# Attention scores as three 64-row products per head pair instead of two stacked 128-row products

## What is computed

```python
def cross_attend(q, k, v):
    n, t, _ = q.shape
    q = q.reshape(n, t, C_HEADS, C_HEAD_DIM)
    s = jnp.einsum('nthd,nshd->nhts', q, k.astype(q.dtype)).astype(jnp.float32) * (C_HEAD_DIM ** -0.5)
    p = jax.nn.softmax(s, axis=-1).astype(q.dtype)
    o = jnp.einsum('nhts,nshd->nthd', p, v.astype(q.dtype))
    return o.reshape(n, t, C_WIDTH)
```

## Time and profile before

| | us |
|---|---|
| median of 3 runs | 405.94 |
| profiled execution | 405.82 |
| its span | 404.1 |
| TensorE matmul busy | 396.3 (2406 instructions) |
| weight loads busy | 371.2 (2406) |
| DVE / ACT / POOL busy | 221.7 / 201.3 / 125.9 |
| granted TensorE clock, mean | 0.998 |

### The profile page before, as it was taken

The page is one execution under the profiler, slowest core; times in us unless marked ns, Lnnn a source line. Parts: engine busy times, 40 slices in busy tenths (PEclk is TensorE's granted clock), DMA queues, the critical chain, the costliest instruction groups (busy, mean ns, idle before and its releaser), DMA issues.

```text
span 404.1 us, 6121 instructions
## 1 busy us (share of the span) xinstructions
PE 396.3 (98%) x2406; PEld 371.2 (92%) x2406; DVE 221.7 (55%) x306; ACT 201.3 (50%) x339; POOL 125.9 (31%) x73
## 2 busy tenths in 40 slices
PE   8999999999999999999999999999999999999994
PEld 8999899999999999999999999999998688888883
DVE  4998696534377668557499734945546241111112
ACT  5974737655446536668694228448163231122220
POOL 2024732232333333203470304205024224444420
PEclk9999999999999999999999999999999999999999
DMA  7993040111012011100350501404342302321122
GB/s 256 411 415 136 0 157 2 54 52 52 0 52 57 6 45 53 52 2 0 115 199 3 208 2 54 156 2 138 107 138 102 105 1 104 104 103 68 72 73 104
DMA packets 13061, 37.96 MB, mean 94 GB/s; under 512 B 2112, under 2 KB 2632, under 8 KB 12912
## 3 DMA queue, kind: packets, MB, share of 16 engines
q1 hardware_dynamic: 13040, 37.68, 26.3%
HBM read 32.84 MB, written 4.83 MB: 93 GB/s over the span
## 4 chain that ended last, share of the span: by engine, by line
PE 95%; DMA 2%; SPq 1%; DVE 1%; ACT 0%; issue 0%; DVEq 0%
PE ps L385 52%; PE ps L655 22%; PE ps L447 3%; DMA mixT<-in_xT 2%; PE ps L589 2%; PE ps L497 2%; PE ps L567 2%; PE ps L555 2%; PE ps L475 1%; PE ps L477 1%; PE ps L489 1%; PE ps L488 1%; PE ps L666 1%; PE ps L668 1%; PE ps L624 1%; PE ps L539 1%
## 5 line engine op out<-in xcount | busy, mean ns | idle before, releaser
L385 PE MATMUL ps<-x_hi,w_hi 128*128 128x344 f32 x456 | 148.8, 326 | 0.5 <-DVE x_lo L1123 0.5
L385 PE MATMUL ps<-x_hi,w_lo 128*128 128x344 f32 x456 | 145.7, 319 | 0.0
L385 PE MATMUL ps<-x_lo,w_hi 128*128 128x344 f32 x456 | 145.5, 319 | 0.0
L385 PEld LDWEIGHTS ps<-x_hi,w_hi 128*128 128x128 f32 x456 | 85.8, 188 | 1.0 <-DVE x_lo L1123 0.8
L385 PEld LDWEIGHTS ps<-x_lo,w_hi 128*128 128x128 f32 x456 | 85.7, 188 | 0.1
L385 PEld LDWEIGHTS ps<-x_hi,w_lo 128*128 128x128 f32 x456 | 85.7, 188 | 0.0
L985 POOL TENSOR_TENSOR w_lo<-w_stage,w_hi 128x1024 fp32r<-128x1024 f32 x17 | 41.7, 2456 | 137.4 <-ACT w_hi L692 127.3
L655 PE MATMUL ps<-x_hi,w_hi 128*128 128x512 f32 x128 | 50.6, 395 | 0.0
L655 PE MATMUL ps<-x_lo,w_hi 128*128 128x512 f32 x128 | 50.5, 394 | 0.0
L655 PE MATMUL ps<-x_hi,w_lo 128*128 128x512 f32 x128 | 50.5, 394 | 0.0
L1092 DVE TENSOR_TENSOR zT<-ps,rstdB 128x344 f32<-128x344 f32 x33 | 16.8, 513 | 34.0 <-PE ps L385 34.0
(11 more groups left out here) (231 smaller groups left out, 650.0 us busy)
## 6 DMA issues: line engine op xcount, KB each, us to landing
w_stage<-in_w_tiles SPq DMA_DIRECT2D x17, 512.0 KB, 3.3
mixT<-in_xT SPq DMA_DIRECT2D x8, 516.0 KB, 8.1
x_ring<-in_x_all SPq DMA_DIRECT2D x8, 512.0 KB, 4.0
o_y<-zT SPq DMA_DIRECT2D x7, 512.0 KB, 2.9
zT<-in_w_out SPq DMA_DIRECT2D x5, 512.0 KB, 4.5
zT<-in_w_mem SPq DMA_DIRECT2D x4, 512.0 KB, 10.9
zT<-in_kcT SPq DMA_DIRECT2D x8, 256.0 KB, 4.0
zT<-in_vc SPq DMA_DIRECT2D x8, 256.0 KB, 5.6
```

Of the source, the lines that this page charges most:

```text
L385: last = pe.matmul(ps[:, bank, 0:GN], w[:, slot, wk], xx[:, k, cols], start=(x == 0 and n == 0), stop=(x == KT - 1 and n == 2))
```

## The change

The stacked copies go. `k_hi`, `k_lo`, `q_hi` and `q_lo` keep the natural layout (both heads of a tile on their own 64 partitions), each made by one 128-partition instruction. A score is three matmuls over 64 rows, hi x hi, hi x lo and lo x hi (the product of the two low parts is left out). Within a tile `t` the two heads alternate, head 0 on rows 0 to 63 into bank 3 and head 1 on rows 64 to 127 into bank 4. A pass has 2 x 3 x 2 = 12 matmuls. The waits count one instruction where they counted two or four, and POOL's wait on itself goes. Each of the four new views takes 512 columns of `z_r`; nothing is placed in `x_r` for the keys any more.

```diff
--- before.py
+++ after.py
@@ -158,11 +158,10 @@
 
 
         z_r, x_r = over("z_r", Z0 + 8 * TT, [P, 3 * TT]), over("x_r", XR0, [P, 2 * TT])
-        k_hh = z_r[:, 0:1024].rearrange("p (a b n) -> p a b n", a=2, b=2)
-        q_st = z_r[:, 1024:2048].rearrange("p (u a b n) -> p u a b n", u=2, a=2, b=2)
+        k_hi, k_lo = (z_r[:, 512 * n:512 * (n + 1)].rearrange("p (t m) -> p t m", t=2) for n in range(2))
+        q_hi, q_lo = (z_r[:, 512 * n:512 * (n + 1)].rearrange("p (u t n) -> p u t n", u=2, t=2) for n in (2, 3))
         v_z = [t.rearrange("p (h n) -> p h n", h=NH) for t in (
             z_r[:, 2 * TT:2 * TT + NH * 3 * HD], x_r[:, 0:NH * 3 * HD])]
-        k_ll = x_r[:, TT:TT + 1024].rearrange("p (a b n) -> p a b n", a=2, b=2)
         xc_hi, xc_lo = (z_r[:, 0:TT], z_r[:, 2 * TT:3 * TT], s_r1[:, :]), x_r[:, 0:TT]
         strips = (x_r[:, TT:2 * TT], s_r1[:, :], x_r[:, TT:2 * TT])
         probsT_hi = over("probsT_hi", PT0, [P, 1024])
@@ -459,8 +458,8 @@
             gemm(3, 1, 1)
             gemm(3, 2, 1)
 
-            pe.wait_ge(khi_done, 4)
-            pe.wait_ge(klo_done, 4)
+            pe.wait_ge(khi_done, 1)
+            pe.wait_ge(klo_done, 1)
             pe.wait_ge(vlo_done, 4)
             pe.wait_ge(const_set, 9)
 
@@ -481,14 +480,15 @@
             with pe.Fori(0, 4) as i:
                 for u in range(2):
                     m, s = i * 2 + (ATT0 + u), i * 2 + u
-                    pe.wait_ge(qc_done, s * 2 + 2)
+                    pe.wait_ge(qc_done, s + 1)
                     for t in range(2):
-                        for hh in range(2):
-                            out = ps[:, 3 + hh, t * NM:(t + 1) * NM]
-                            pe.matmul(out, q_st[:, u, hh, t, :], k_hh[:, hh, t, :], start=True, stop=False)
-                            last = pe.matmul(out, q_st[:, u, hh, t, :], k_ll[:, hh, t, :], start=False, stop=True)
-                            if t == 1:
-                                last.then_inc(sc_done, 1)
+                        for n, (q, k) in enumerate(((q_hi, k_hi), (q_hi, k_lo), (q_lo, k_hi))):
+                            for hh in range(2):
+                                r = slice(hh * HD, (hh + 1) * HD)
+                                last = pe.matmul(ps[:, 3 + hh, t * NM:(t + 1) * NM], q[r, u, t, :], k[r, t, :],
+                                                 start=(n == 0), stop=(n == 2))
+                                if t == 1 and n == 2:
+                                    last.then_inc(sc_done, 1)
                     gemm(m, 0, u)
                     gemm(m, 1, u)
                     for b in range(2):
@@ -748,19 +748,13 @@
 
             def split_q(c0, slot):
 
-                for hh in range(2):
-                    r = slice(hh * HD, (hh + 1) * HD)
-                    act.activation(q_st[r, slot, hh, :, :], zT[r, 0:2, bass.ds(c0, P)], ACT.Copy).then_inc(qhi_done, 1)
+                act.activation(q_hi[:, slot, :, :], zT[:, 0:2, bass.ds(c0, P)], ACT.Copy).then_inc(qhi_done, 1)
 
             act.wait_ge(q_done, 2)
             split_q(0, 0)
             act.wait_ge(kTp_done, 1)
-            for src in range(2):
-                for hh in range(2):
-                    r, to = slice(hh * HD, (hh + 1) * HD), (hh + src) % 2
-                    act.activation(k_hh[to * HD:(to + 1) * HD, hh, :, :],
-                                   ps[r, 5, :].rearrange("p (t n) -> p t n", t=2), ACT.Copy,
-                                   scale=-HD ** -0.5).then_inc(khi_done, 1)
+            act.activation(k_hi, ps[:, 5, :].rearrange("p (t n) -> p t n", t=2), ACT.Copy,
+                           scale=-HD ** -0.5).then_inc(khi_done, 1)
             for j in range(2):
                 act.wait_ge(z_used, 3 * (T_GC + j + 1))
                 act.activation(sig_c[j], mixT[:, 6 + j, :], ACT.Sigmoid).then_inc(gcsig_done, 1)
@@ -1012,14 +1006,11 @@
             with pool.Fori(0, 4) as i:
                 for u in range(2):
                     m, s = i * 2 + (ATT0 + u), i * 2 + u
-                    pool.wait_ge(qhi_done, s * 2 + 2)
+                    pool.wait_ge(qhi_done, s + 1)
 
                     pool.wait_ge(wlo_done, m + 1)
-                    for hh in range(2):
-                        r, to = slice(hh * HD, (hh + 1) * HD), slice((1 - hh) * HD, (2 - hh) * HD)
-                        pool.tensor_tensor(q_st[to, u, hh, :, :], zT[r, 0:2, bass.ds(i * (2 * P) + u * P, P)],
-                                           q_st[r, u, hh, :, :].bitcast(F), ALU.subtract).then_inc(qc_done, 1)
-                        pool.wait_ge(qc_done, s * 2 + (hh + 1))
+                    pool.tensor_tensor(q_lo[:, u, :, :], zT[:, 0:2, bass.ds(i * (2 * P) + u * P, P)],
+                                       q_hi[:, u, :, :].bitcast(F), ALU.subtract).then_inc(qc_done, 1)
                     low_w(m + 1, 1 - u)
 
             pool.wait_ge(wsT_in, 16)
@@ -1159,13 +1150,9 @@
                 for odd in range(2):
                     dve.tensor_tensor(z[:, odd, :, 0:HD] if odd else z[:, odd, :, 2 * HD:3 * HD], v[:, odd, :, :],
                                       z[:, odd, :, HD:2 * HD].bitcast(F), ALU.subtract).then_inc(vlo_done, 1)
-            dve.wait_ge(khi_done, 4)
-            for hh in range(2):
-                r = slice(hh * HD, (hh + 1) * HD)
-                for to in range(2):
-                    dve.scalar_tensor_tensor(k_ll[to * HD:(to + 1) * HD, hh, :, :],
-                                             ps[r, 5, :].rearrange("p (t n) -> p t n", t=2), -HD ** -0.5,
-                                             k_hh[r, hh, :, :].bitcast(F), ALU.mult, ALU.subtract).then_inc(klo_done, 1)
+            dve.wait_ge(khi_done, 1)
+            dve.scalar_tensor_tensor(k_lo, ps[:, 5, :].rearrange("p (t n) -> p t n", t=2), -HD ** -0.5,
+                                     k_hi.bitcast(F), ALU.mult, ALU.subtract).then_inc(klo_done, 1)
 
             def gate_c(j):
                 dve.wait_ge(gcsig_done, j + 1)
```

## The result

The changed kernel takes 407.39 us (407.33 to 407.59, 7 runs) against 405.94 us before on the same chip: a ratio of 1.0034, 95% interval 1.0024 to 1.0044. It is slower by 1.45 us where 407.1 was forecast. The profiled execution took 407.35 us, its span is 405.6 us, 1.5 us longer than before.

A forecast was written before the change was run, and what follows sets the result against it. TensorE's own stream was taken to bound the kernel. Per pass, -0.23 us from paired scores and +0.39 from form changes give +0.16, over eight passes +1.25: 405.82 + 1.25 = 407.1 us, range 403.8 to 412.4.

The forecast's parts named there:

- TensorE's stream alone sets the end: From 15.15 to 398.7 us TensorE is busy without a hole; changes to its stream move the end one for one.
- Part 1: Score matmuls: six overlapping half-row pairs at 0.117 us gain 0.23 us per pass; one after another they lose 0.39.
- C: Rival, score blocks: pairs overlap and the form change is free, -0.23 us per pass, 403.9 us; chance 0.16.
- B: Rival, score blocks: weight loads queue and form changes cost, +0.78 us per pass, 412.0 us; chance 0.25.
- D: Rival, score blocks: weight loads queue, form change free, +0.39 us per pass, 408.9 us; chance 0.08.
- Part 2: Between w_in products and scores: changing from 128 rows to 64 and back costs 0.39 us per pass.
- bound of 0: Low end for the form changes: none, since lines 666 and 668 alternate 64 and 32 columns without a gap.
- Part 3: ACT, DVE and POOL: fewer copies and subtractions free time but end no TensorE wait, so worth nothing.
- The sum: Eight passes of -0.23 + 0.39 = +0.16 us give +1.25 us on the path, 407.1 us.
- E: Rival, score blocks: half-row loads aren't hidden under any matmul, +2.02 us per pass, 422 us; chance 0.05.

## Why the prediction was right, point by point

- *TensorE's stream alone sets the end.* Right. The other engines lost 17 us of busy time together and gave nothing back, and the experiments moved by what their TensorE streams moved.
- *Part 1, a pair costs one full matmul.* Right: steps of 0.12 us, head 1 free (407.32 without it), 0.116 us per pair by the run with hi x hi alone. It was a choice between two ends, not a derivation: the prediction gave this one 0.62 between forecast and C, and no row of the kernel before has products of two row halves side by side. In the changed kernel's second block two loads have started 0.07 us after its start, where a second load of the same half comes after 0.11. Why both halves load together no run shows. B's 412.0 and D's 408.9 fell by the run with one head. B's "every 128-column load" has an exception: in the trace before, a load of line 624 follows another within 0.07 us, at 250.20.
- *Part 2, in and out cost 0.39 us per pass.* Right in place and in size: 0.41 by doubling it and by the hi x hi run, 0.40 by the passes of the two traces (0.167 us more per pass, and 0.23 that six slots save on eight). The way in is what line 614 showed, and both ends cost about 0.20 us: 0.91 us for six steps of 0.117, and 7.72 for 7.52 us behind them. The load gap of 0.2 us that was forecast at each end is 0.22 us at the way in and 0.14 at the way out (80.47 + 0.77 to 81.38). That the array runs empty in these gaps is the prediction's reading; what the rows show is the loader standing idle and the first load behind not hidden. Its times for columns to leave, 107 ns for 256 and 0.03 us for 32, stand in no row and no run shows them: measured were 0.117 us from one score matmul to the next, and about 0.20 us for the way out as a whole. The bound of 0 by lines 666 and 668 fell: they change columns, and the run with half of the stationary columns (ratio 0.9999) shows no price for them in fp32r. C's 403.9 fell with it. There was some luck in it: line 614 is fp32, and line 599, fp32 with all 128 rows, had the same gap, so the trace before couldn't say whether the rows, the type or the 32 columns made it. The runs settle it for fp32r rows: 64 of them cost 0.41 us per pass, 128 in the same kernel left no gap (0.01 us from the last product to the first score load).
- *Part 3, no price elsewhere.* Right; ACT lost about what was forecast (5.4 for about 5 us), DVE and POOL more (3.2 for 2.1, 8.5 for 6). On POOL the forecast went by the median of 732 ns, but the two subtractions of 64x256 had a mean of 912 each (the longest took 1820), and the single one of 128x256 has a mean of 778.
- *The sum.* 1.25 us forecast, 1.45 measured. The traces put about 1.35 of it into the eight passes, 0.1 more than the sum has; what is left, about 0.1, lies ahead of the attention, where the prediction expected no difference, and its cause is open. It is less than the 0.5 us by which runs of the kernel before differ (405.81 to 406.34).
- *E* (422 us) fell by the same rows: within a block the steps are 0.12 us, where E has 0.21; its 0.107 us for a matmul's 256 columns stands in no row either.

## What to carry to other kernels

On a path that TensorE sets, count its slots, and add about 0.20 us at each end for a change of active rows (measured with 64 of 128 rows in fp32r; a 256-column step is 0.117): halving K pays only if enough paired work follows before the array goes back, here more than 0.41 / 0.117 = 3.5 slots saved per block, where two were. Removing copies on engines that wait anyway bought nothing here (17 us of busy time less, 1.45 us slower). Two half-row streams need not alternate instruction by instruction: three in a row of one half cost nothing (407.36 for 407.39 us) and six cost three steps (410.31 us); nothing between was run.

## What the runs showed of the hardware that I had not expected

- Matmuls of different row halves didn't keep the order of the file: with three of one half ahead, the other half's first load started 10 ns behind the block's first, and the last two matmuls started 10 ns apart. So the sentence on the kernel before that each engine's instructions run in the order of the file doesn't hold for TensorE across row halves; within one half no row speaks against it. Whether a semaphore on the last matmul in the file alone could come too early was not tried: with six in turn the file's last one also started last, 0.35 us behind head 0's last.
- The reach is short: with six in turn the second half began three steps late (0.35 us in the trace, 0.36 us per pass in the time).
- A change of active rows, 64 for 128, cost 0.41 us in and out, a change of active columns, 64 for 128, nothing (ratio 0.9999), both with fp32r operands; in plain fp32, 32 columns with all rows had a gap of 0.21 us.
